# Tokens loaded after the modulation weights, and the first normalisation done by halves of the tokens, in a one-core hybrid attention and expert block

## The chip, the cores and the metric

The kernel runs on one core of a Trainium2 chip. The metric is the device time of the program in microseconds (us), the median of several executions. PE is TensorE, DVE is VectorE, ACT is ScalarE, POOL is GpSimd and SP is SyncE, which only issues DMAs here.

## The reference

The program is one residual block on 1024 tokens of width 1024: a LayerNorm of the input, a modulation by a vector `c`, a mixer (delta-rule linear attention beside sliding-window attention), and a mixture of experts. The change lies in the first lines of it and in the key columns of the first projection:

```python
h = layer_norm(x, ln_in_g, ln_in_b)
ada = jax.nn.silu(c) @ w_ada[l] + b_ada[l]
sh1, sc1, gt1, sh2, sc2, gt2 = jnp.split(ada, 6, axis=-1)
u = h * (1.0 + sc1[:, None, :]) + sh1[:, None, :]
proj = u @ w_in                # k_b: the 128 key columns of the window attention
```

`layer_norm` takes mean and variance over the 1024 channels of each token, so a token's normalised row needs nothing of other tokens.

## The kernel before

The program is a row of stages (`prepare`, `attention`, `project`, `delta_rule`, `merge`, `route`, `experts`). Each stage is a block with one hand-written instruction list for each engine; at its end all engines meet at a barrier. The change touches `prepare` alone.

`prepare` makes `u`, the modulated tokens, transposed (channels on the partitions) and as a sum of two float16 numbers, high and low, in `m.u`. Its work:

- SP issues all loads on one queue: a small table, the vectors, the tokens `x` in four pieces of two token chunks (1 MB each, L270), the first 2048 columns of `w_ada` in five pieces (three of 2 MB, two of 1 MB, L272), the first slice of the dense weights (`load_dense(…, 0)`, L170 with 1 MB and L171 with 16 columns in 64-byte runs), small rows, the rest of the table and the second dense slice. A token chunk is 128 tokens, one a partition.
- DVE takes the moments of the eight token chunks (`bn_stats` L390, two for each chunk, `bn_aggr` L393), ACT the square root (L355), DVE reciprocal and shift (L396, L398), and ACT normalises the eight chunks in place (L359, counted in `z_ok`).
- The modulation: PE multiplies `silu(c)` with the columns 0 to 1023 of `w_ada` as the pieces land (`ada(k)`, L295), DVE sums the columns 1024 to 2047 into `part` (L404, L407). PE turns both into columns (L335, L302), and DVE makes scale and shift `m.mod` (L414 to L421, `ada_ok`).
- The loop of 16 steps, n = 0 to 15. In step n PE transposes four 128x128 blocks into a PSUM bank (`turn(n)`, L311): eight channel groups k by two halves of the tokens, of 512 each. A bank serves four steps, so `turn(n)` waits until step n-4 has been read (`hi_ok`). ACT reads the bank of an even step twice (L371, L373) and makes the high part of an odd step (L377) from what DVE read (L427). DVE then subtracts to get the low part of either (L433, `ut_ok`). PE multiplies the key columns with the result, three matmuls a step (`keys(n)`, L321). PE's order is `turn(n)`, `keys(n-4)`, `turn(n+1)`, `keys(n-3)` and so on. Before, n goes over both halves of one k and then the next k, and turns 0 to 2 stand between `ada(5)` and `ada(6)`.
- ACT and DVE split the first dense slice into high and low (L182, L190); `keys(0)` waits for the low part. DVE does it after step 1.
- At n = 8 PE also makes the rows of the relative bias (L346); DVE copies them after step 9, and SP stores them for `attention`.

`attention` begins behind the barrier with PE's value products (L559), which need all of `u`.

Of the kernel before, what the change touches and what calls it, by code (L numbers as in the profile page):

```python
# [11 lines left out]
ALU = mybir.AluOpType  # L12
ACT = mybir.ActivationFunctionType
# [211 lines left out]
def prepare(nc, m, a):  # L225
# [4 lines left out]
    with ExitStack() as ctx:  # L230
# [33 lines left out]
        @block.sync  # L264
        def _(sp):
            sp.dma_start(m.table[:, 0:2 * P], a["table"][:, 0:2 * P]).then_inc(table_in, 16)
            sp.dma_start(vec_rows[:], a["vectors"]).then_inc(vecs_in, 16)
            sp.dma_start(conv_rows[:], a["conv_rows"]).then_inc(vecs_in, 16)
            for c in range(4):
                sp.dma_start(x[:, 2 * c:2 * c + 2, :], x_view[:, 2 * c:2 * c + 2, :]).then_inc(x_in[c], 16)  # L270
            for n, ks in enumerate(GROUPED):
                sp.dma_start(wada[:, ks[0]:ks[-1] + 1, :], w_view[:, ks[0]:ks[-1] + 1, 0:2 * D]).then_inc(wada_in[n], 16)  # L272
            load_dense(m, a, sp, 0)
            sp.dma_start(m.small[:], a["small"].to_broadcast([P, 72])).then_inc(small_in, 16)
            sp.dma_start(rel[:], a["rel_bias"]).then_inc(rel_in, 16)
            sp.dma_start(m.table[:, 2 * P:], a["table"][:, 2 * P:]).then_inc(rest_in, 16)
            load_dense(m, a, sp, 1)
            sp.wait_ge(bias_rows, 1)
            sp.dma_start(m.bias_dram.rearrange("i h x -> h i x"), rel_rows[:].rearrange("h (o x) -> h o x", o=1).to_broadcast([QH, COPIES, 320])
                         ).then_inc(m.bias_out, 16)  # L280
            sp.wait_ge(small_in, 16)
            sp.wait_ge(m.bias_out, 16)

        @block.tensor
        def _(pe):
            pe.wait_ge(table_in, 16)
            pe.wait_ge(vecs_in, 32)
            pe.transpose(ps[:, 0, 0:VEC_N], vec_rows[:], m.const("ident")[0:VEC_N, 0:VEC_N])
            pe.transpose(ps[:, 0, VEC_N:VEC_N + 96], conv_rows[:], m.const("ident")[0:96, 0:96]).then_inc(vecs_t, 1)
            pe.wait_ge(vecs_ok, 1)  # L290

            def ada(k):
                pe.wait_ge(wada_in[k // 2 if k < 6 else k - 3], 16)
                for n in range(ON_TENSOR):
                    last = pe.matmul(ps[0:1, ROW[n], :], m.silu_c[:, k:k + 1], wada[:, k, n * 512:(n + 1) * 512], start=(k == 0), stop=(k == KC - 1))  # L295
                    if k == KC - 1:
                        last.then_inc(ada_mm, 1)

            def columns(n):
                pe.wait_ge(row_ok[n], 1)  # L300
                for j in range(4 * n, 4 * n + 4):
                    last = pe.transpose(ps[:, 6, j:j + 1], ada_row[0:1, j * P:(j + 1) * P], m.const("ident")[0:1, 0:1])  # L302
                last.then_inc(cols_mm, 1)

            def turn(n):

                k, half = n // 2, n % 2
                if n >= 4:
                    pe.wait_ge(hi_ok, n - 3)
                for c in range(4):  # L310
                    last = pe.transpose(ps[:, 2 + n % 4, c * P:(c + 1) * P], x[:, 4 * half + c, k * P:(k + 1) * P], m.const("ident"))  # L311
                last.then_inc(zt, 1)

            def keys(n):

                k, half = n // 2, n % 2
                if n == 0:
                    pe.wait_ge(m.w_lo, 4)
                pe.wait_ge(ut_ok, n + 1)
                for t, (wp, up) in enumerate(PASSES):  # L320
                    last = pe.matmul(ps[:, half, :], m.w16[:, 0, wp, k, 0:P], m.u[:, up, k, half * 512:half * 512 + 512],  # L321
                                     start=(k == 0 and t == 0), stop=(k == KC - 1 and t == 2))
                if k == KC - 1:
                    last.then_inc(m.k_mm, 1)

            pe.wait_ge(silu_ok, 1)
            for k in range(KC):
                ada(k)
                if k == KC - 3:
                    pe.wait_ge(z_ok, TC)  # L330
                    for n in range(3):
                        turn(n)
            pe.wait_ge(part_ok, 1)
            for j in range(KC):
                last = pe.matmul(ps[:, 6, KC + j:KC + j + 1], part[:, j * P:(j + 1) * P], m.const("ones")[:, 0:1], start=True, stop=True)  # L335
            last.then_inc(cols_mm, 1)
            for n in range(ON_TENSOR):
                columns(n)
            turn(3)
            for n in range(4, 2 * KC):  # L340
                turn(n)
                keys(n - 4)
                if n == 8:
                    pe.wait_ge(rel_in, 16)
                    pe.wait_ge(rest_in, 16)
                    pe.matmul(ps[0:QH, 7, 0:320], rel[:], m.const("one_hot", BUCKETS), start=True, stop=True).then_inc(bias_mm, 1)  # L346
            for n in range(2 * KC - 4, 2 * KC):
                keys(n)

        @block.scalar  # L350
        def _(act):
            act.wait_ge(vecs_ok, 1)
            nc.scalar.activation(sig_c[:], m.vec("c"), ACT.Sigmoid).then_inc(sig_ok, 1)
            act.wait_ge(var_ok, 1)
            nc.scalar.activation(std[:], mv[:, :, 1], ACT.Sqrt, bias=eps[:, 0:1]).then_inc(std_ok, 1)  # L355

            act.wait_ge(shift_ok, 1)
            for c in range(TC):
                nc.scalar.activation(x[:, c, :], x[:, c, :], ACT.Identity, scale=rstd[:, c:c + 1], bias=shift[:, c:c + 1]).then_inc(z_ok, 1)  # L359
            act.wait_ge(ada_mm, 1)  # L360
            nc.scalar.copy(ada_row[:, 0:512], ps[0:1, ROW[0], :]).then_inc(row_ok[0], 1)
            split_dense_high(nc, m, act, 0)

            act.wait_ge(ada_ok, 1)
            for n in range(2 * KC):
                k, half = n // 2, n % 2
                if half == 0:
                    act.wait_ge(zt, n + 1)
                    if n >= 4:
                        act.wait_ge(ut_ok, n - 3)  # L370
                    nc.scalar.activation(u32[:, n % 4, :], ps[:, 2 + n % 4, :], ACT.Identity,  # L371
                                         scale=m.mod[:, 0, k:k + 1], bias=m.mod[:, 1, k:k + 1]).then_inc(u32_even, 1)
                    nc.scalar.activation(m.u[:, 0, k, 0:512], ps[:, 2 + n % 4, :], ACT.Identity,  # L373
                                         scale=m.mod[:, 0, k:k + 1], bias=m.mod[:, 1, k:k + 1]).then_inc(hi_ok, 1)
                else:
                    act.wait_ge(u32_odd, k + 1)
                    nc.scalar.copy(m.u[:, 0, k, 512:T], u32[:, n % 4, :]).then_inc(hi_ok, 1)  # L377

        @block.vector
        def _(dve):  # L380
# [3 lines left out]
            nc.vector.tensor_copy(m.vecs[:], ps[:, 0, 0:VEC_N + 96]).then_inc(vecs_ok, 1)  # L384
            dve.wait_ge(sig_ok, 1)
            nc.vector.tensor_tensor(m.silu_c[:], sig_c[:], m.vec("c"), ALU.mult).then_inc(silu_ok, 1)
            for c in range(TC):
                dve.wait_ge(x_in[c // 2], 16)
                for s in range(2):
                    step(nc.vector.bn_stats(stats[:, c, s, :], x[:, c, s * 512:(s + 1) * 512]))  # L390
            step.settle()
            for c in range(TC):
                last = nc.vector.bn_aggr(mv[:, c, :], stats[:, c, :, :])  # L393
            last.then_inc(var_ok, 1)
            dve.wait_ge(std_ok, 1)
            step(nc.vector.reciprocal(rstd[:], std[:]))  # L396
            step.settle()
            nc.vector.scalar_tensor_tensor(shift[:], mv[:, :, 0], -1.0, rstd[:], ALU.mult, ALU.mult).then_inc(shift_ok, 1)  # L398

            for k in range(KC):  # L400
                dve.wait_ge(wada_in[k // 2 if k < 6 else k - 3], 16)
                piece = wada[:, k, ON_TENSOR * 512:]
# [17 lines left out]
            step.settle()  # L420
            nc.vector.tensor_tensor(m.mod[:, 1, :], m.mod[:, 1, :], ada[:, 0:KC], ALU.add).then_inc(ada_ok, 1)  # L421
            dve.wait_ge(ada_ok, 1)
            for n in range(2 * KC):
                k, half = n // 2, n % 2
                if half == 0:
                    dve.wait_ge(zt, n + 2)
                    nc.vector.tensor_scalar(u32[:, n % 4 + 1, :], ps[:, 3 + n % 4, :], m.mod[:, 0, k:k + 1], m.mod[:, 1, k:k + 1],  # L427
                                            ALU.mult, ALU.add).then_inc(u32_odd, 1)
                    dve.wait_ge(u32_even, k + 1)
                else:  # L430
                    dve.wait_ge(u32_odd, k + 1)
                dve.wait_ge(hi_ok, n + 1)
                nc.vector.tensor_tensor(m.u[:, 1, k, half * 512:half * 512 + 512], u32[:, n % 4, :], m.u[:, 0, k, half * 512:half * 512 + 512],  # L433
                                        ALU.subtract).then_inc(ut_ok, 1)
                if n == 1:
                    split_dense_low(nc, m, dve, 0)
                if n == 9:
                    dve.wait_ge(bias_mm, 1)
                    nc.vector.tensor_copy(rel_rows[:], ps[0:QH, 7, 0:320]).then_inc(bias_rows, 1)
# [2176 lines left out]
```

## Time and profile before

| | us |
|---|---|
| three runs | 2009.5, 2012.44, 2005.38 |
| median | 2009.5 |
| the profiled execution | 2011.88 |
| its span, first to last instruction | 2010.0 |
| PE busy / DVE busy / ACT busy | 1830.9 / 1441.6 / 1066.0 |
| last key product of `prepare` starts its run of 15 | 63.66 |
| first value product of `attention` | 67.70 |

Times of the trace count from the start of the span. `prepare` is the first 67 us of it. A row of the trace's timeline has start, length, engine, line, operation, tiles and count, and in brackets how long the engine was idle before and what ended that.

### The profile page before, as it was taken

What the parts mean: (1) busy time and instruction counts of PE and PEld (TensorE: products, weight loads), DVE (VectorE), ACT (ScalarE), POOL (GpSimd) and SP (SyncE); (2) the same over time, 40 slices, a digit from 0 to 9 for tenths busy, and PEclk for the clock granted to TensorE, in tenths of its full rate; (3) what the DMA queues carried; (4) which work ended last, traced back from release to release, by engine and by line L of the source; (5) the groups of instructions that cost most, each with busy time, mean ns of one, the idle gap of its engine ahead of it and who ended that gap; (6) DMA issues with size and microseconds to landing.
All of it is one profiled execution on the core that took longest, in us unless ns stands there. A gap on an engine that the chain in (4) does not pass through costs nothing. (4 is left out here: it accounts for less than half of the span.)

```text
span 2010.0 us, 35245 instructions
## 1 busy us (share of the span) xinstructions
PE 1830.9 (91%) x14108; PEld 1041.1 (52%) x14108; DVE 1441.6 (72%) x1820; ACT 1066.0 (53%) x1292; POOL 358.7 (18%) x230
## 2 busy tenths in 40 slices
PE   4988869999978999989999999379999999999965
PEld 1655554444448999964444455334444444444432
DVE  5455555777776666627575778779999888888938
ACT  3455552355343334324333411169889888888944
POOL 0000000111101122100000000024444444444410
PEclk9999979999999999999999999589999999999988
DMA  8500007573545313006223221379999999999935
GB/s 318 101 22 22 1 1 282 189 251 126 179 107 128 81 50 93 7 14 189 77 80 94 75 81 73 130 292 409 403 406 410 403 394 401 391 396 384 383 135 207
DMA packets 161716, 391.32 MB, mean 195 GB/s; under 512 B 25371, under 2 KB 102804, under 8 KB 132910
## 3 DMA queue, kind: packets, MB, share of 16 engines
q1 hardware_dynamic: 146574, 357.87, 49.2%
q0 software_dynamic: 15008, 31.56, 4.1%
q8 instruction: 96, 1.57, 0.3%
q14 instruction: 38, 0.31, 0.1%
HBM read 361.68 MB, written 48.68 MB: 204 GB/s over the span
## 5 line engine op out<-in xcount | busy, mean ns | idle before, releaser
L2268 PE MATMUL ps<-w_gate_up_split,gathered_t 128*128 128x512 f16 x1728 | 387.8, 381 | 8.0 <-ACT gathered_t L2342 3.8
L2434 DVE SCALAR_TENSOR_TENSOR w_gate_up_split<-w_staged,w_gate_up_split 128x2048 f16<-128x2048 f32 x144 | 327.5, 2289 | 56.1 <-ACT w_gate_up_split L2333 55.0
L2333 ACT ACTIVATE w_gate_up_split<-w_staged 128x2048 f16<-128x2048 f32 x144 | 274.2, 1908 | 66.5 <-PEq L144 31.4
L2268 PEld LDWEIGHTS ps<-w_gate_up_split,gathered_t 128*128 128x128 f16 x1728 | 167.3, 98 | 209.0 <-ACT gathered_t L2342 10.5
L219 PE MATMUL ps<-u_transposed,w_gates_split 128*128 128x512 f16 x1152 | 253.9, 382 | 5.0 <-PEq L144 3.0
L825 PE MATMUL ps<-u_transposed,w_dense_split 128*128 128x512 f16 x1152 | 250.5, 379 | 1.8 <-DVE w_dense_split L190 1.0
L2295 PE MATMUL ps<-w_down_split,hidden_t 128*128 128x512 f16 x864 | 193.8, 381 | 7.8 <-ACT hidden_t L2379 4.7
L219 PEld LDWEIGHTS ps<-u_transposed,w_gates_split 128*128 128x128 f16 x1152 | 113.1, 98 | 145.5 <-issue 13.0
L825 PEld LDWEIGHTS ps<-u_transposed,w_dense_split 128*128 128x128 f16 x1152 | 111.9, 98 | 142.4 <-issue 7.1
L2434 DVE SCALAR_TENSOR_TENSOR w_down_split<-w_staged,w_down_split 128x2048 f16<-128x2048 f32 x72 | 164.2, 2289 | 21.1 <-ACT w_down_split L2333 20.8
L2333 ACT ACTIVATE w_down_split<-w_staged 128x2048 f16<-128x2048 f32 x72 | 137.1, 1907 | 46.1 <-DMA w_staged<-in_w_down 30.3
L2295 PEld LDWEIGHTS ps<-w_down_split,hidden_t 128*128 128x128 f16 x864 | 82.9, 98 | 104.3 <-ACT hidden_t L2379 6.5
L190 DVE SCALAR_TENSOR_TENSOR w_dense_split<-w_dense_ring,w_dense_split 128x512 f16<-128x512 f32 (+2 forms) x29 | 41.0, 1413 | 109.7 <-ACT w_dense_split L182 109.7
L1348 ACT ACTIVATE level_product<-ps 128x256 f32<-128x256 f32 x80 | 30.7, 384 | 145.8 <-PE ps L1223 143.8
L2224 POOL DMA_INDIRECT slots_scratch<-block_output,slot_row_now x36 | 49.1, 1365 | 327.4 <-ACT block_output L2351 319.0
L1737 ACT ACTIVATE gate_sigmoids<-ps 128x1024 f32<-128x1024 f32 x24 | 24.5, 1023 | 143.0 <-PE ps L219 143.0
L498 PE MATMUL ps<-u_transposed,w_dense_split 128*128 128x512 f16 x384 | 90.0, 380 | 0.0
L952 DVE SCALAR_TENSOR_TENSOR delta_output<-w_gates_split,vector_columns,delta_output 128x1024 f32<-128x1024 f32 x66 | 83.8, 1283 | 7.2 <-ACT delta_output L888 5.6
L1671 PE MATMUL ps<-w_out_split,delta_output 128*128 128x512 f16 x384 | 84.0, 379 | 0.0
L2210 POOL DMA_INDIRECT gathered<-u_scratch,slot_token_now x34 | 76.9, 2263 | 29.0 <-POOL slot_token_now L2207 29.0
L1085 POOL DMA_DIRECT2D qkv_scratch<-delta_output x20 | 11.1, 553 | 392.5 <-ACT delta_output L895 392.5
L2220 POOL COPY slot_row_now<-slot_rows_index 128x1 uint32 (+1 forms) x36 | 76.6, 2128 | 0.1
(364 smaller groups left out, 2934.7 us busy)
## 6 DMA issues: line engine op xcount, KB each, us to landing
w_staged<-in_w_gate SPq DMA_DIRECT2D x72, 1024.0 KB, 12.2
w_staged<-in_w_up SPq DMA_DIRECT2D x72, 1024.0 KB, 11.6
w_staged<-in_w_down SPq DMA_DIRECT2D x72, 1024.0 KB, 12.0
w_dense_ring<-in_w_in SPq DMA_DIRECT2D x17, 1024.0 KB, 7.6
w_ada_ring<-in_w_ada SPq DMA_DIRECT2D x8, 2048.0 KB
w_gates_ring<-in_w_in SPq DMA_DIRECT2D x24, 512.0 KB, 6.4
qkv_scratch<-delta_output POOLq DMA_DIRECT2D x20, 512.0 KB, 4.0
attention_output<-qkv_scratch SPq DMA_DIRECT2D x8, 1024.0 KB, 5.9
```

The lines of the kernel that those rows point to most:

```text
L219: last = pe.matmul(m.ps[:, 2 * j + half, :], m.gate16[n % 2][:, j, wp, k, :], m.u[:, up, k, half * 512:half * 512 + 512], start=(t == 0), ...
L498: last = pe.matmul(ps[:, bank, :], w16[:, i % 2, wp, k, (j % 2) * P:(j % 2 + 1) * P], m.u[:, up, k, half * 512:half * 512 + 512], start=(t ...
L825: last = pe.matmul(ps[:, 2 * b + half, :], w16[:, (FIRST + p) % 2, i, k, b * P:(b + 1) * P], m.u[:, j, k, half * 512:half * 512 + 512], st ...
L952: last = nc.vector.scalar_tensor_tensor(acc[:, b, :], raw[:, b, 1 + t:1 + t + T], conv[:, t, n:n + 1], acc[:, b, :], ALU.mult, ALU.add)
L1671: last = pe.matmul(ps[:, y_bank(c) + half, :], merged(k, op)[:, c * P:(c + 1) * P], m.w_out[:, wp, k, half * 512:half * 512 + 512], start= ...
L2210: pool.indirect_dma_start(xg[:, s].rearrange("p h d -> p (h d)"), None, m.u2_dram.rearrange("t h d -> t (h d)"), bass.IndirectOffsetOnAxis ...
L2220: nc.gpsimd.tensor_copy(row[:, s:s + 1], m.slot_row[:, bass.ds(n, 1)]).then_inc(S("row_ready"), 1)
L2224: pool.indirect_dma_start(m.y_dram, bass.IndirectOffsetOnAxis(ap=row[:, s:s + 1], axis=0), y[:, s, :], None, bounds_check=2 * T - 1, oob_i ...
L2268: last = pe.matmul(ps[:, GU[s] + j, :], xt[:, s, xp, k, :], w16[:, j, wp, k, :], start=(k == 0 and t == 0), stop=(k == KC - 1 and t == 2))
L2295: last = pe.matmul(ps[:, 6 + half, :], ht[:, s, hp, k, :], wd16[:, wp, k, half * 512:half * 512 + 512], start=(k == 0 and t == 0), stop=(k ...
L2333: nc.scalar.activation(split(kind, 0, int(q)), staged(m, kind, int(q)), ACT.Identity, scale=W_SCALE).then_inc(hi_ok[kind + q], 1)
L2434: nc.vector.scalar_tensor_tensor(split(kind, 1, int(q)), staged(m, kind, int(q)), W_SCALE, split(kind, 0, int(q)), ALU.mult, ALU.subtract) ...
```

## The change

The loads are issued in another order: `w_ada`, the first dense slice, then the tokens. PE does all of `ada(k)` without turns between them. Moments, square root, shift and normalising are done for token chunks 0 to 3 and again for chunks 4 to 7. The loop's steps run over k for the first half of the tokens (n = 0 to 7) and then over k for the second half (n = 8 to 15); the moments of the second half stand on DVE before step 2, its square root on ACT before step 4, its shift on DVE and its normalising on ACT before step 6. `turn(0)` waits for four normalised chunks, `turn(8)` for eight. The split of the first dense slice stands before the loop on DVE.

```diff
@@ sync
-            for c in range(4):
-                sp.dma_start(x[:, 2 * c:2 * c + 2, :], x_view[:, 2 * c:2 * c + 2, :]).then_inc(x_in[c], 16)
             for n, ks in enumerate(GROUPED):
                 sp.dma_start(wada[:, ks[0]:ks[-1] + 1, :], w_view[:, ks[0]:ks[-1] + 1, 0:2 * D]).then_inc(wada_in[n], 16)
             load_dense(m, a, sp, 0)
+            for c in range(4):
+                sp.dma_start(x[:, 2 * c:2 * c + 2, :], x_view[:, 2 * c:2 * c + 2, :]).then_inc(x_in[c], 16)
@@ tensor
             def turn(n):
-                k, half = n // 2, n % 2
+                k, half = n % KC, n // KC
+                if k == 0:
+                    pe.wait_ge(z_ok, 4 * (half + 1))
...
             for k in range(KC):
                 ada(k)
-                if k == KC - 3:
-                    pe.wait_ge(z_ok, TC)
-                    for n in range(3):
-                        turn(n)
...
-            turn(3)
+            for n in range(4):
+                turn(n)
@@ scalar
-            act.wait_ge(var_ok, 1)
-            nc.scalar.activation(std[:], mv[:, :, 1], ACT.Sqrt, bias=eps[:, 0:1]).then_inc(std_ok, 1)
...
+            def tokens(half):
+                act.wait_ge(shift_ok, half + 1)
+                for c in range(4 * half, 4 * half + 4):
+                    nc.scalar.activation(x[:, c, :], x[:, c, :], ACT.Identity, scale=rstd[:, c:c + 1], bias=shift[:, c:c + 1]).then_inc(z_ok, 1)
...
             split_dense_high(nc, m, act, 0)
+            roots(0)
+            tokens(0)
             act.wait_ge(ada_ok, 1)
             for n in range(2 * KC):
-                k, half = n // 2, n % 2
-                if half == 0:
+                k, half = n % KC, n // KC
+                if n == 4:
+                    roots(1)
+                if n == 6:
+                    tokens(1)
+                if n % 2 == 0:
@@ vector
+            moments(0)
+            shifts(0)
+            split_dense_low(nc, m, dve, 0)
             for n in range(2 * KC):
-                k, half = n // 2, n % 2
-                if half == 0:
+                k, half = n % KC, n // KC
+                if n == 2:
+                    moments(1)
+                if n == 6:
+                    shifts(1)
+                if n % 2 == 0:
...
-                if n == 1:
-                    split_dense_low(nc, m, dve, 0)
```

SP's queue, from the fourth load on (`attention_output` is the tile that holds the tokens here). Before:

```order
L270 DMA attention_output<-in_x 128x2x1024 x4
L272 DMA w_ada_early<-in_w_ada 128x2x2048 x3
L272 DMA w_ada_early<-in_w_ada 128x2048 x2
L170 DMA w_dense_ring<-in_w_in 128x8x256
L171 DMA w_dense_ring<-in_w_in 128x8x16
L274 DMA small_rows<-in_small 128x72
```

Now:

```order
L270 DMA w_ada_early<-in_w_ada 128x2x2048 x3
L270 DMA w_ada_early<-in_w_ada 128x2048 x2
L170 DMA w_dense_ring<-in_w_in 128x8x256
L171 DMA w_dense_ring<-in_w_in 128x8x16
L273 DMA attention_output<-in_x 128x2x1024 x4
L274 DMA small_rows<-in_small 128x72
```

The four token loads have moved behind seven others.

DVE, around the moments. Before, they stand ahead of the modulation's partial sums:

```order
L386 TENSOR_TENSOR silu_c<-sigmoid_c,vector_columns 128x8
L390 BN_STATS ln_stats<-attention_output 128x6 x16
L393 BN_AGGR ln_mean_var<-ln_stats 128x2 x8
L396 RECIPROCAL ln_rstd<-ln_std 128x8
L398 SCALAR_TENSOR_TENSOR ln_minus_mean_rstd<-ln_mean_var,ln_rstd 128x8
L404 TENSOR_SCALAR ada_early_partial<-w_ada_early,silu_c 128x1024
L407 SCALAR_TENSOR_TENSOR ada_early_partial<-w_ada_early,silu_c,ada_early_partial 128x1024 x7
L412 COPY ada_early_row<-ps 1x512
```

Now, behind the modulation, from the first half's moments into the loop:

```order
L400 BN_STATS ln_stats<-attention_output 128x6 x8
L403 BN_AGGR ln_mean_var<-ln_stats 128x2 x4
L409 RECIPROCAL ln_rstd<-ln_std 128x4
L411 SCALAR_TENSOR_TENSOR ln_minus_mean_rstd<-ln_mean_var,ln_rstd 128x4
L190 SCALAR_TENSOR_TENSOR w_dense_split<-w_dense_ring,w_dense_split 128x2176
L448 TENSOR_SCALAR u_float<-ps,modulation 128x512
L454 TENSOR_TENSOR u_transposed<-u_float,u_transposed 128x512 x2
L400 BN_STATS ln_stats<-attention_output 128x6 x8
L403 BN_AGGR ln_mean_var<-ln_stats 128x2 x4
L448 TENSOR_SCALAR u_float<-ps,modulation 128x512
L454 TENSOR_TENSOR u_transposed<-u_float,u_transposed 128x512 x2
L448 TENSOR_SCALAR u_float<-ps,modulation 128x512
```

L448 and L454 are the loop's operations (L427 and L433 before); eight moments of the second half now stand inside it, after one pair of steps.

ACT, the loop. Before, all eight chunks are normalised ahead of it (L359):

```order
L355 ACTIVATE ln_std<-ln_mean_var,ln_eps 128x8
L359 ACTIVATE attention_output<-attention_output,ln_minus_mean_rstd,ln_rstd 128x1024 x8
L361 COPY ada_early_row<-ps 1x512
L182 ACTIVATE w_dense_split<-w_dense_ring 128x2176
L371 ACTIVATE u_float<-ps,modulation 128x512
L373 ACTIVATE u_transposed<-ps,modulation 128x512
L377 CAST u_transposed<-u_float 128x512
```

Now, from the loop's first step:

```order
L380 ACTIVATE u_float<-ps,modulation 128x512
L382 ACTIVATE u_transposed<-ps,modulation 128x512
L386 CAST u_transposed<-u_float 128x512
L380 ACTIVATE u_float<-ps,modulation 128x512
L382 ACTIVATE u_transposed<-ps,modulation 128x512
L386 CAST u_transposed<-u_float 128x512
L356 ACTIVATE ln_std<-ln_mean_var,ln_eps 128x4
L380 ACTIVATE u_float<-ps,modulation 128x512
L382 ACTIVATE u_transposed<-ps,modulation 128x512
L386 CAST u_transposed<-u_float 128x512
L361 ACTIVATE attention_output<-attention_output,ln_minus_mean_rstd,ln_rstd 128x1024 x4
L380 ACTIVATE u_float<-ps,modulation 128x512
```

Four of the eight normalisings now stand inside the loop, after three pairs of steps.

## Rows read from the trace of the kernel before

**Rows 1.** The page: its first line, and the chain that ended last.

```profile
span 2010.0 us, 35245 instructions
...
PE 14%; DMA 12%; DVE 5%; ACT 2%; issue 1%; SPq 0%; ACTq 0%; POOLq 0%; DVEq 0%
```

**Rows 2.** Timeline of SP: when each load was issued, and for how long.

```profile
2.04 2.14 SPq L270 DMA_DIRECT2D attention_output<-in_x  x4
4.22 7.71 SPq L272 DMA_DIRECT2D w_ada_early<-in_w_ada  x5
...
13.26 18.71 SPq L171 DMA_DIRECT2D w_dense_ring<-in_w_in  x1
32.01 4.05 SPq L274 DMA_DIRECT2D small_rows<-in_small  x1
```

**Rows 3.** Issue to landing of the loads of L270, then L272, then L171.

```profile
DMA to landing us min/median/max: 6.4/9.5/12.6
...
DMA to landing us min/median/max: 16.9/25.4/27.2
...
DMA to landing us min/median/max: 26.0/26.0/26.0
```

**Rows 4.** Timeline of DVE: moments, dense split, and one step of the loop.

```profile
8.46 10.14 DVE L390 BATCH_NORM_STATS2 ln_stats<-attention_output 128x6 f32<-128x512 f32 x16 [1.00 <-DMA attention_output<-in_x]
...
18.64 0.71 DVE L393 BATCH_NORM_AGGREGATE ln_mean_var<-ln_stats 128x2 f32<-128x12 f32 x8
...
45.83 2.42 DVE L190 SCALAR_TENSOR_TENSOR w_dense_split<-w_dense_ring,w_dense_split 128x2176 f16<-128x2176 f32 x1
...
57.35 0.81 DVE L427 TENSOR_SCALAR u_float<-ps,modulation 128x512 f32<-128x512 f32 x1 [0.70 <-PE ps L311]
```

**Rows 5.** Timeline of ACT: the normalising, and the loop's first read.

```profile
20.16 9.16 ACT L359 ACTIVATE attention_output<-attention_output,ln_minus_mean_rstd,ln_rstd 128x1024 f32<-128x1024 f32 x8 [0.47 <-DVE ln_minus_mean_rstd L398]
...
43.07 0.78 ACT L371 ACTIVATE u_float<-ps,modulation 128x512 f32<-128x512 f32 x1 [1.67 <-DVE modulation L421]
```

**Rows 6.** Timeline of PE: modulation products, turns and key products.

```profile
21.23 9.57 PE L295 MATMUL ps<-w_ada_early,silu_c 128*1 128x512 f32 x16 [14.59 <-DMA w_ada_early<-in_w_ada]
...
36.08 3.59 PE L295 MATMUL ps<-w_ada_early,silu_c 128*1 128x512 f32 x8
...
48.31 1.46 PE L321 MATMUL ps<-u_transposed,w_dense_split 128*128 128x512 f16 x3 [2.62 <-DVE w_dense_split L190]
49.56 1.06 PE L311 MATMUL ps<-table,attention_output 128*128 128x128 f32 x4
...
51.69 1.06 PE L311 MATMUL ps<-table,attention_output 128*128 128x128 f32 x4
...
58.88 0.60 PE L311 MATMUL ps<-table,attention_output 128*128 128x128 f32 x4
...
59.97 0.60 PE L311 MATMUL ps<-table,attention_output 128*128 128x128 f32 x4
...
63.66 3.72 PE L321 MATMUL ps<-u_transposed,w_dense_split 128*128 128x512 f16 x15
```

**Rows 7.** Groups of DVE from 43 to 67.5 us: count, busy us, mean ns.

```profile
L433 DVE TENSOR_TENSOR u_transposed<-u_float,u_transposed 128x512 f16<-128x512 f32 x16 | 10.9, 688 | 1.8 <-ACT u_transposed L377 0.8 <-ACT u_transposed L373 0.7
L427 DVE TENSOR_SCALAR u_float<-ps,modulation 128x512 f32<-128x512 f32 x8 | 6.5, 806 | 2.5 <-PE ps L311 2.4
```

**Rows 8.** Windows of PE alone: stretch, length, busy (count), granted clock, DMA.

```profile
43.00:44.00 1.00, 0.00 (x0) 0.72 1.00 319
...
53.00:54.00 1.00, 1.00 (x6) 0.66 0.00 0
```

**Rows 9.** Window of all engines, 22 to 23 us: PE first; clock third last.

```profile
22.00:23.00 1.00, 1.00 (x3) 0.24 (x2) 1.00 (x1) 1.00 (x2) 0.00 (x0) 1.00 0.95 393
```

**Rows 10.** Timeline of ACT: its first instruction behind the barrier.

```profile
67.67 0.60 ACT L587 ACTIVATE k_transposed<-ps 128x512 f32<-128x512 f32 x1 [1.97 <-PEq L230]
```

More of the change, by code:

```diff
@@ L353, in _, with roots @@
             nc.scalar.activation(sig_c[:], m.vec("c"), ACT.Sigmoid).then_inc(sig_ok, 1)
-            act.wait_ge(var_ok, 1)
-            nc.scalar.activation(std[:], mv[:, :, 1], ACT.Sqrt, bias=eps[:, 0:1]).then_inc(std_ok, 1)
-            act.wait_ge(shift_ok, 1)
-            for c in range(TC):
-                nc.scalar.activation(x[:, c, :], x[:, c, :], ACT.Identity, scale=rstd[:, c:c + 1], bias=shift[:, c:c + 1]).then_inc(z_ok, 1)
+            def roots(half):
+                cs = slice(4 * half, 4 * half + 4)
+                act.wait_ge(var_ok, half + 1)
+                nc.scalar.activation(std[:, cs], mv[:, cs, 1], ACT.Sqrt, bias=eps[:, 0:1]).then_inc(std_ok, 1)
+            def tokens(half):
+                act.wait_ge(shift_ok, half + 1)
+                for c in range(4 * half, 4 * half + 4):
+                    nc.scalar.activation(x[:, c, :], x[:, c, :], ACT.Identity, scale=rstd[:, c:c + 1], bias=shift[:, c:c + 1]).then_inc(z_ok, 1)
             act.wait_ge(ada_mm, 1)
@@ L362, in _ @@
             split_dense_high(nc, m, act, 0)
+            roots(0)
+            tokens(0)
             act.wait_ge(ada_ok, 1)
             for n in range(2 * KC):
-                k, half = n // 2, n % 2
-                if half == 0:
+                k, half = n % KC, n // KC
+                cols = slice(half * 512, half * 512 + 512)
+                if n == 4:
[3 more added lines that the diff above has]
+                if n % 2 == 0:
                     act.wait_ge(zt, n + 1)
@@ L372, in _ @@
                                          scale=m.mod[:, 0, k:k + 1], bias=m.mod[:, 1, k:k + 1]).then_inc(u32_even, 1)
-                    nc.scalar.activation(m.u[:, 0, k, 0:512], ps[:, 2 + n % 4, :], ACT.Identity,
+                    nc.scalar.activation(m.u[:, 0, k, cols], ps[:, 2 + n % 4, :], ACT.Identity,
                                          scale=m.mod[:, 0, k:k + 1], bias=m.mod[:, 1, k:k + 1]).then_inc(hi_ok, 1)
                 else:
-                    act.wait_ge(u32_odd, k + 1)
-                    nc.scalar.copy(m.u[:, 0, k, 512:T], u32[:, n % 4, :]).then_inc(hi_ok, 1)
+                    act.wait_ge(u32_odd, n // 2 + 1)
+                    nc.scalar.copy(m.u[:, 0, k, cols], u32[:, n % 4, :]).then_inc(hi_ok, 1)
         @block.vector
@@ L386, in _, with moments, shifts @@
             nc.vector.tensor_tensor(m.silu_c[:], sig_c[:], m.vec("c"), ALU.mult).then_inc(silu_ok, 1)
[L387 to L398, printed above, removed]
+            def moments(half):
+                for c in range(4 * half, 4 * half + 4):
+                    dve.wait_ge(x_in[c // 2], 16)
+                    for s in range(2):
+                        step(nc.vector.bn_stats(stats[:, c, s, :], x[:, c, s * 512:(s + 1) * 512]))
+                step.settle()
+                for c in range(4 * half, 4 * half + 4):
+                    last = nc.vector.bn_aggr(mv[:, c, :], stats[:, c, :, :])
+                last.then_inc(var_ok, 1)
+            def shifts(half):
+                cs = slice(4 * half, 4 * half + 4)
+                dve.wait_ge(std_ok, half + 1)
+                step(nc.vector.reciprocal(rstd[:, cs], std[:, cs]))
+                step.settle()
+                nc.vector.scalar_tensor_tensor(shift[:, cs], mv[:, cs, 0], -1.0, rstd[:, cs], ALU.mult, ALU.mult).then_inc(shift_ok, 1)
+            dve.wait_ge(silu_ok, 1)
             for k in range(KC):
@@ L422, in _ @@
             dve.wait_ge(ada_ok, 1)
+            moments(0)
+            shifts(0)
+            split_dense_low(nc, m, dve, 0)
             for n in range(2 * KC):
-                k, half = n // 2, n % 2
-                if half == 0:
+                k, half = n % KC, n // KC
+                if n == 2:
[3 more added lines that the diff above has]
+                if n % 2 == 0:
                     dve.wait_ge(zt, n + 2)
-                    nc.vector.tensor_scalar(u32[:, n % 4 + 1, :], ps[:, 3 + n % 4, :], m.mod[:, 0, k:k + 1], m.mod[:, 1, k:k + 1],
+                    nc.vector.tensor_scalar(u32[:, n % 4 + 1, :], ps[:, 3 + n % 4, :], m.mod[:, 0, k + 1:k + 2], m.mod[:, 1, k + 1:k + 2],
                                             ALU.mult, ALU.add).then_inc(u32_odd, 1)
-                    dve.wait_ge(u32_even, k + 1)
+                    dve.wait_ge(u32_even, n // 2 + 1)
                 else:
-                    dve.wait_ge(u32_odd, k + 1)
+                    dve.wait_ge(u32_odd, n // 2 + 1)
                 dve.wait_ge(hi_ok, n + 1)
```

## The prediction

> **What bounds the kernel now.** I read the page first. The chain that ended last runs through the experts and names nothing of `prepare` [rows 1], so it can't price this change; but it can't excuse it either. `prepare` ends at a barrier, ACT's first instruction behind it waited for PE's queue [rows 10], and from there PE works on `u`. So what `prepare` ends later or earlier moves everything behind it by as much, and the question is where 63.66 + 3.72 = 67.4 us, the end of the last key product [rows 6], goes.
>
> Next I read the queues of the first 67 us. The four token loads were issued from 2.04 us on; the first landed after 6.4 us, at 8.4, the last (issued at 3.5) after 12.6 us, at 16.1 [rows 2, 3], so 1 MB takes 2.55 us. The 8 MB of `w_ada` fill the time until 36.1, where the last products of L295 start [rows 6], and the first dense slice is complete at 13.26 + 26.0 = 39.3 [rows 2, 3]. The tokens' whole preparation hides in that: moments from 8.46 for 10.14 us, normalising from 20.16 for 9.16 us [rows 4, 5], while the weights still arrive. At 39.3 nothing of the tokens is left but transposing. The modulation is ready at 43.07, 3.4 us after the last L295 ends at 39.7, and the loop starts there [rows 5, 6]. It takes 67.4 - 43.1 = 24.3 us, of which DVE is busy 10.9 + 6.5 + 2.4 us [rows 4, 7]. **The bound of `prepare` is bytes until 39.3, then the loop, a ring in which PE, ACT and DVE all take part.**
>
> **The change, part by part.** *The loads.* The bytes are the same, so the tokens and the weights exchange places: with the tokens last they land at 31.7, 34.2, 36.8 and 39.3, counted back from 39.3 by 2.55. The last piece of `w_ada` lands 4 x 2.55 = 10.2 us earlier, at 25.9. One doubt is SP: it sat 18.7 us in issuing the 64-byte runs of L171 and 4.05 in the load behind it, until 36.06, which is when `w_ada` had landed [rows 2]. The token loads now stand behind L171. By the same picture the first is out at about 26, 3 us before its turn comes, so I take no loss; if the queue does run dry, I bound that by one token load, 0 to 2.5 us.
>
> *The modulation.* It is ready at about 27.8 + 3.4 = 31.2, instead of 43.07. That is the gain that the change reaches for. But at 31.2 no token has landed, so it is worth nothing by itself.
>
> *The first half.* Two token loads have landed at 34.2. Four `bn_stats` at 0.63 (10.14 / 16) follow: 36.8. From the first `bn_aggr` to the first normalising took 18.64 to 20.16 = 1.5 us with eight, so 1.2 with four: 38.0. Four normalisings at 1.145 (9.16 / 8): **42.6** [rows 4, 5]. There the loop can begin. That is only 0.5 us ahead of 43.07. DVE's dense split (2.42 us [rows 4]) now lies beside the normalising, costs nothing, and would show only if the normalising were 2 us shorter; before, PE waited 2.62 us for it [rows 6]. That is a gain inside the loop.
>
> *Inside the loop.* Here the other half of the tokens' work now stands, with nothing to hide it. I walk the chain:
> - Turns 0 and 1. PE has been idle since about 31. The turns start 0.9 apart and run 1.06 at the low clock (1.2 GHz), 0.6 at the high one (2.4 GHz) [rows 6, 8]. I take the low one: 44.7.
> - DVE's first pair of steps, 0.81 + 2 x 0.69 = 2.2 [rows 7]: 46.9.
> - The second half's moments, 8 x 0.63 + 4 x 0.09 = 5.4: 52.3. PE runs out of work at about 50, since `keys(2)` needs step 2 of DVE.
> - Pair 2/3, 2.2, then pair 4/5, 2.4 with a wait for ACT: 56.9. ACT's square root (0.3) fits between.
> - Shift on DVE 0.3: 57.2. Then ACT normalises, 4.6: **61.8**. Neither pair 6/7 on ACT nor `turn(8)` on PE can start before; PE, done with `keys(3)` at 55.7, idles 6 us.
> - PE's list then holds `turn(8)`, `keys(4)`, the bias product, `turn(9)`. A turn and its keys start to start are 2.13 us low (49.56 to 51.69) and 1.09 high (58.88 to 59.97) [rows 6]. At the low clock this list takes 2.13 + 1.3 + 1.2 = 4.7: 66.5, and DVE can read the bank.
> - Before, DVE's reading for steps 8 and 9 began at 57.35 [rows 4] and `prepare` ended 10.0 us later. The same steps remain: 76.5, and 0.6 for one more turn at the low clock: **77.1**.
>
> Sum: 77.1 - 67.4 = **+9.7 us**. Within it: start -0.5, dense split out -2.4, moments, shift and normalising in +10.3, the low clock +2 to +3, and small waits for the rest. The profiled execution was 2011.88, so I expect 2021.6 from such a one; the median of the runs shown is 2.4 lower, 2009.5, so the median becomes 2019.2.
>
> *The clock.* The price of the low clock is the least certain term. The granted clock fell at about 43.7, with PE idle from 42.7, and rose at about 53.7, after turns and keys without a gap from 49 on [rows 8]. Two rows disagree on the start. At 22 us the granted clock reads 1.00 after 14.6 us of idle [rows 9], but the sixteen matmuls from 21.23 take 0.60 each where the eight of 36.08 take 0.45 [rows 6]. I believe the matmuls. By the row of the clock alone, PE would be high after any early wait and the sum would be nearer +7. The Trainium skill, "TensorE: Matmul & The Clock Gate", section "Loop structure matters more than you think", says that a long wait for a DMA between matmuls drops PE to the low clock; by it turn 0 and `turn(8)` both start low, as in my sum. It speaks against this change, which adds both waits. The same page says in "Seeing it yourself" that recorded clock events can be unreliable, and the two rows above show such a case.
>
> **The rivals.**
> 1. *The clock stays high behind the 6 us wait at 56 to 62.* `turn(9)` is then done at 64.5 and the end is 74.5: +7.1, or 2016.6. With turns 0 and 1 high too, +6.2. For it: rows 9. Against: the fall at 43.7 after far less.
> 2. *The clock stays low to the end of the loop.* After 66.5, six turns and some eleven groups of key products at 1.04 extra for a turn and its keys, partly hidden by DVE, add 5 to 9 us: +15 to +19, or 2026.5. For it: with steps in half-filled pairs PE has gaps. Against: before, the clock rose while the same list was running [rows 6, 8].
> 3. *Not slower: the tokens land out of the order of issue.* All loads go over one queue and the same 16 engines. If the small rows and the 64-byte runs let the token loads overtake, so that they land 5 us before my times, the first half starts at 37.6, and each step up to the 61.8 follows by 5: +4.7, or 2014.2. It decides from about 4 us earlier on, when the rest is under 6.0 us. For it: SP's long issue of L171 [rows 2] shows that the queue doesn't take all loads alike. Against: the loads of L270 and L272 landed one behind the other at an even pace [rows 3]. The Trainium skill, "DMA: Bandwidth & Descriptors", section "Queues, rings and completion order", says that completion is not in order of issue for DMAs that use few engines; by it this could happen only beside a load of few engines.
> 4. *The reorder doesn't do what it says: SP holds the token loads back* behind L171, so that the queue runs dry by 2.5 to 5 us. Every step after moves with it: +12.2 to +14.7, or 2023.
>
> **How the numbers follow.** A measurement of this kernel can tell about 0.3% from no change, which is 6.0 us: slower means over 2015.5. Chances: my forecast (+9.7) 0.52, rival 1 0.20, rival 2 0.10, rival 3 0.08, rival 4 0.10. The three runs shown spread by 7 us, so a median can stray by 2 to 3. Forecast, 2 and 4 give slower nearly always, rival 1 in two of three cases, rival 3 hardly. That makes slower 0.77, same 0.21, and 0.02 for faster, since no row lets the loop both start earlier and lose its stalls. The likeliest time is 2019.2. The range runs from rival 1 less 2.6 of spread, 2014.0, to rival 4 with some spread, 2026.0; it leaves out most of rival 2 and part of rival 3.
>
> **What would show it.** Right: `w_ada`'s last landing near 26 and the tokens' last near 39.3; the modulation at about 31; the first turn at 42.6 and not before; between it and the barrier a stretch of DVE `bn_stats` (about 47 to 52) and one of ACT normalising (57 to 62) with PE idle in both; the first L559 at about 77.4 instead of 67.7. Behind that, stages of the same length as before. Wrong: a first turn well before 42; the turn behind ACT's normalising in 0.6 us instead of 1.06; a barrier before 73; or a later stage that takes the delay in.

## The result, and the profile after

| | before | changed |
|---|---|---|
| median of six runs, us | 2012.99 | 2022.42 |
| range of the six | 2005.38 to 2015.13 | 2020.65 to 2025.8 |
| profiled execution / its span | 2011.88 / 2010.0 | 2023.0 / 2021.1 |
| first key copy of ACT behind the barrier | 67.67 | 77.66 |

The ratio is 1.005, with a 95% interval of 1.0037 to 1.0063: the change makes the kernel slower by 9.4 us, where 9.7 were forecast. The runs of before have moved as well: its median of six is 3.5 us above that of the first three, so 2022.42 stands higher than the 2019.2 of the forecast although the difference is right.

SP's timeline of the changed kernel (start, length, engine, line, what is loaded, count):

```profile
2.04 2.59 SPq L270 DMA_DIRECT2D w_ada_early<-in_w_ada  x5
4.67 0.47 SPq L170 DMA_DIRECT2D w_dense_ring<-in_w_in  x1
5.18 14.83 SPq L171 DMA_DIRECT2D w_dense_ring<-in_w_in  x1
20.05 7.95 SPq L273 DMA_DIRECT2D attention_output<-in_x  x4
```

From issue to landing, the token loads of L273:

```profile
DMA to landing us min/median/max: 8.7/11.2/12.3
```

The last token load was issued at 27.3 and landed at 39.6 (27.3 + 12.3). Before, the last byte of the dense slice landed at about that time, 39.3 [rows 2, 3]. The loads have only changed places. DVE's timeline shows what each load released:

```profile
25.67 1.28 DVE L421 SCALAR_TENSOR_TENSOR ada_early_partial<-w_ada_early,silu_c,ada_early_partial 128x1024 f32<-128x1024 f32 x1 [1.03 <-DMA w_ada_early<-in_w_ada]
...
30.82 0.17 DVE L435 TENSOR_TENSOR modulation<-modulation,ada_early 128x8 f32<-128x8 f32 x1
32.05 4.96 DVE L400 BATCH_NORM_STATS2 ln_stats<-attention_output 128x6 f32<-128x512 f32 x8 [1.06 <-DMA attention_output<-in_x]
...
45.69 1.50 DVE L454 TENSOR_TENSOR u_transposed<-u_float,u_transposed 128x512 f16<-128x512 f32 x2
47.11 4.84 DVE L400 BATCH_NORM_STATS2 ln_stats<-attention_output 128x6 f32<-128x512 f32 x8
...
63.08 1.29 DVE L454 TENSOR_TENSOR u_transposed<-u_float,u_transposed 128x512 f16<-128x512 f32 x2 [5.38 <-ACT u_transposed L382]
66.36 0.81 DVE L448 TENSOR_SCALAR u_float<-ps,modulation 128x512 f32<-128x512 f32 x1 [1.99 <-PE ps L313]
```

The modulation is ready at 31.0 (30.82 + 0.17), 12 us earlier than before [rows 5], and nothing can use it yet. The second `bn_stats` row is the second half's moments between two steps of the loop. ACT's timeline has the normalisings, the second one inside the loop too:

```profile
38.24 4.63 ACT L361 ACTIVATE attention_output<-attention_output,ln_minus_mean_rstd,ln_rstd 128x1024 f32<-128x1024 f32 x4 [0.44 <-DVE ln_minus_mean_rstd L411]
44.14 0.78 ACT L380 ACTIVATE u_float<-ps,modulation 128x512 f32<-128x512 f32 x1 [1.26 <-PE ps L313]
...
57.02 4.63 ACT L361 ACTIVATE attention_output<-attention_output,ln_minus_mean_rstd,ln_rstd 128x1024 f32<-128x1024 f32 x4 [1.11 <-DVE ln_minus_mean_rstd L411]
```

PE's timeline answers to [rows 6]:

```profile
42.93 4.53 PE L313 MATMUL ps<-table,attention_output 128*128 128x128 f32 x20 [12.84 <-ACT attention_output L361]
...
53.74 0.82 PE L323 MATMUL ps<-u_transposed,w_dense_split 128*128 128x512 f16 x3 [3.61 <-DVE u_transposed L454]
...
61.70 1.11 PE L313 MATMUL ps<-table,attention_output 128*128 128x128 f32 x4 [6.06 <-ACT attention_output L361]
62.61 1.49 PE L323 MATMUL ps<-u_transposed,w_dense_split 128*128 128x512 f16 x3
...
73.96 3.40 PE L323 MATMUL ps<-u_transposed,w_dense_split 128*128 128x512 f16 x15
77.68 12.28 PE L578 MATMUL ps<-w_dense_split,u_transposed 128*128 128x144 f16 x192 [0.32 <-PEq L230]
```

PE waits three times: 12.84 us for the first half of the tokens, 3.61 for DVE's moments, 6.06 for ACT's second normalising. The first wait is the earlier modulation, unused. It costs little against before, since the loop's first read on ACT is at 44.14 where it was at 43.07 [rows 5]. The other two carry the result. Before, PE waited in the loop for 2.62 us [rows 6] and 1.85 us:

```profile
44.57 1.11 PE L311 MATMUL ps<-table,attention_output 128*128 128x128 f32 x4 [1.85 <-ACT u_transposed L373]
```

The granted clock of the changed kernel, in windows of PE (length, busy, granted clock, DMA share, GB/s; 0.50 is 1.2 GHz, 1.00 is 2.4 GHz, and a value between them is a window in which it changed):

```profile
54.00:56.00 2.00, 1.64 (x10) 1.00 0.00 0
56.00:58.00 2.00, 0.00 (x0) 1.00 0.00 0
58.00:60.00 2.00, 0.00 (x0) 0.65 0.00 0
60.00:62.00 2.00, 0.29 (x2) 0.50 0.00 0
...
66.00:68.00 2.00, 2.00 (x8) 0.50 0.00 0
68.00:70.00 2.00, 2.00 (x12) 0.79 0.03 6
```

It falls at about 58.6, in the last wait, and the turns and keys from 61.70 to about 68.8 run at 1.2 GHz.

The last product of `prepare` ends at 77.36 against 67.38, +9.98 us. Behind the barrier the delay stays: the first load of the expert weights, on SP, starts at

```profile
1283.20 0.81 SPq L2099 DMA_DIRECT2D w_staged<-in_w_gate  x2
```

which is 8.9 us later than before (1274.34).

### The profile page after: what moved, and what is told of

It is laid out like the page before. It is cut to its first block and busy times, and to the rows that moved or that the text cites. A ratio compares the mean times of both kernels' runs of the same rounds, so it can differ in the third digit from the quotient of the medians.

```text
span 2021.1 us, 35250 instructions
## 1 busy us (share of the span) xinstructions
PE 1834.0 (91%) x14108; PEld 1043.6 (52%) x14108; DVE 1441.3 (71%) x1822; ACT 1066.0 (53%) x1293; POOL 356.7 (18%) x230
## 5 line engine op out<-in xcount | busy, mean ns | idle before, releaser
L1104 POOL DMA_DIRECT2D qkv_scratch<-delta_output x20 | 11.1, 553 | 401.4 <-ACT delta_output L914 401.4
L621 ACT ACTIVATE scores_biased<-scores_biased,softmax_rows 128x192 f32<-128x192 f32 x128 | 56.5, 446 | 37.9 <-DVE softmax_rows L671 37.9
```

Source lines behind the costliest of these rows:

```text
L621: nc.scalar.activation(sp_[:, t % 2, h, :], sp_[:, t % 2, h, :], ACT.Exp, bias=neg_max[:, t % 2, h:h + 1], accum_out=sums[:, t % 2, h:h + 1])
```

## The experiments

Places in `prepare` are compared by the start of attention's first value product: 67.70 before, 77.68 in the changed kernel.

### The second half ahead of the loop

```diff
 act:     roots(0)
          tokens(0)
+         roots(1)
+         tokens(1)
          for n in range(2 * KC):
-             if n == 4: roots(1)
-             if n == 6: tokens(1)
 dve:     split_dense_low(nc, m, dve, 0)
+         moments(1)
+         shifts(1)
          for n in range(2 * KC):
-             if n == 2: moments(1)
-             if n == 6: shifts(1)
```

> The changed kernel, loads still with the tokens last, but the second half's moments, root, shift and normalising stand ahead of the loop on DVE and ACT. Theory A (what costs is the second half's work standing inside the loop, DVE 5.4 us and ACT 4.6 us in a chain that PE waits for): moments of the second half from 40.5 to 46, normalised at 50.7, the loop's first read near 51, then pairs of steps every 2.2 to 2.5 us; first value product of attention at 68 to 70 against 77.7, so +0.5 to +2.5 us against the kernel before, within 0.3%. Theory B (what costs is that the tokens land last, 23 us later than before): the time stays with the changed kernel, first value product at 76 to 78, +8 to +10 us. Theory C (the low clock behind the 6 us wait is the larger part): the wait is gone, so it can't be told from A by the sum, but A wants the second half's 10 us to vanish from the loop, C only 3 us: 74 to 75.

Measured: 1.0024 of before (1.0014 to 1.0033), median 2018.32. PE's timeline of this run:

```profile
42.58 3.68 PE L313 MATMUL ps<-table,attention_output 128*128 128x128 f32 x16 [12.75 <-ACT attention_output L361]
52.20 1.11 PE L313 MATMUL ps<-table,attention_output 128*128 128x128 f32 x4 [5.95 <-ACT u_transposed L380]
...
70.94 12.28 PE L574 MATMUL ps<-w_dense_split,u_transposed 128*128 128x144 f16 x192 [0.32 <-PEq L230]
```

Same loads, same work, 6.7 us less. Theory B, that late tokens cost all of it whatever the lists do, falls. So does C as the main part: a wait of 5.95 us is still there, ahead of 52.20, with the low clock behind it (the turn took 1.11 us), and the 6.7 us are back all the same. I had written that this wait would be gone, and had left the low clock out of A's number, which came out 0.9 us too low. What is left of the loss against the kernel before is 3.2 us.

### Only the moments ahead

```diff
 dve:     split_dense_low(nc, m, dve, 0)
+         moments(1)
+         shifts(1)
          for n in range(2 * KC):
-             if n == 2: moments(1)
-             if n == 6: shifts(1)
 act:     roots(0)
          tokens(0)
+         roots(1)
          for n in range(2 * KC):
-             if n == 4: roots(1)
```

> The changed kernel with the second half's moments, root and shift ahead of the loop, the normalising of the second half still on ACT before step 6. Theory A: the moments no longer stop DVE inside the loop (5.4 us), but PE still waits for the normalising; first value product at 69.3 if PE's clock stays high behind that wait of about 4 us, at 73 if it drops; so -4.5 to -8.4 us against the changed kernel. Theory B: no more than 1 us less than the changed kernel, since the tokens land as late.

Measured: 1.0021 (1.0011 to 1.0031), first value product at 71.26. That is 6.4 us less than the changed kernel, between A's two ends. PE's wait for the normalising has shrunk from 6.06 us:

```profile
57.04 0.66 PE L313 MATMUL ps<-table,attention_output 128*128 128x128 f32 x4 [2.79 <-ACT attention_output L361]
...
58.99 1.12 PE L313 MATMUL ps<-table,attention_output 128*128 128x128 f32 x4
```

The turn behind the wait is at the high clock (0.66), the next one at the low (1.12), so the clock fell just after. Of the pair, the moments are the dear part: with them and the square root out of the loop, the normalising costs 0.3 us more inside it than ahead of it (71.26 against 70.94), and the two ratios, 1.0021 and 1.0024, can't be told apart.

### Filler in the 6 us wait

```diff
                 turn(n)
                 keys(n - 4)
+                if n == 7:
+                    for _ in range(24):
+                        pe.matmul(ps[:, 6, :], m.w16[:, 0, 0, 0, 0:P], m.u[:, 0, 0, 0:512], start=True, stop=True)
```

> The changed kernel with 24 float16 matmuls into an unused bank put on PE behind the key products of step 3, where it waits 6 us for the second half (they add no work that anybody reads). They take about 5.2 us. Theory C and my sum: the clock stays high at 61.7, turn(8) to turn(9) take 2.4 us less and the next turns 0.5: first value product at 74.3, -3.4 us. If the clock is no part of it: 77.7, no change.

Measured: 1.0039 (1.0024 to 1.0054), first value product at 75.33, -2.35 us against the -3.4 expected. PE's timeline:

```profile
56.56 6.07 PE L344 MATMUL ps<-u_transposed,w_dense_split 128*128 128x512 f16 x24
62.46 0.60 PE L313 MATMUL ps<-table,attention_output 128*128 128x128 f32 x4
...
75.33 12.28 PE L581 MATMUL ps<-w_dense_split,u_transposed 128*128 128x144 f16 x192 [0.32 <-PEq L230]
```

The turn takes 0.60 instead of 1.11, so the clock is a real term. The filler itself took 0.7 us of the gain back: it ran for 6.07 us, not 5.2, since in this execution the clock was low from 54.6 to 58.0, and `turn(8)`, which could have gone at 61.8, started at 62.46.

### The changed lists with the tokens loaded first

```diff
+            for c in range(4):
+                sp.dma_start(x[:, 2 * c:2 * c + 2, :], ...).then_inc(x_in[c], 16)
             for n, ks in enumerate(GROUPED):
                 sp.dma_start(wada[...], w_view[...]).then_inc(wada_in[n], 16)
             load_dense(m, a, sp, 0)
-            for c in range(4):
-                sp.dma_start(x[:, 2 * c:2 * c + 2, :], ...).then_inc(x_in[c], 16)
```

> The changed kernel's instruction lists with the loads in the order of before (tokens, w_ada, dense slice). Theory A, with the moments behind the modulation on DVE and nothing else changed: modulation at about 41.5, moments to 47, first half normalised at 52.4, loop from there with the second half's work in it as in the changed kernel: first value product at 86.7, +9 us against the changed kernel and +19 against the kernel before. Theory B (the late tokens are the cost): it returns to the kernel before, 67 to 70.

Measured: 1.0102 (1.0087 to 1.0117), median 2034.2, first value product at 87.24 where A said 86.7. DVE's timeline shows why:

```profile
41.31 4.84 DVE L400 BATCH_NORM_STATS2 ln_stats<-attention_output 128x6 f32<-128x512 f32 x8
```

PE's timeline has the end of it:

```profile
87.24 12.28 PE L578 MATMUL ps<-w_dense_split,u_transposed 128*128 128x144 f16 x192 [0.32 <-PEq L230]
```

The tokens have been there since 16, but on DVE's list the moments stand behind the modulation, which now ends at 41. Under the changed lists the changed order of loads is worth 9.6 us. The fourth combination, the changed loads under the lists of before, was not run.

### Only the loop's order

```diff
-                k, half = n // 2, n % 2
+                k, half = n % KC, n // KC
```

with the same on PE, ACT and DVE, and nothing else of the change.

> The kernel before with the loop's steps in the changed order alone (all channel groups of the first half, then of the second); loads, norms, split as before. Theory A: the order of the steps in itself costs nothing, as every step has the same work: first value product at 67.7 +- 0.5, same time. If the order costs by itself (the rival that explains the changed kernel by it), up to +10 us.

Measured: 1.0001 (0.9987 to 1.0014):

```profile
66.94 12.28 PE L560 MATMUL ps<-w_dense_split,u_transposed 128*128 128x144 f16 x192 [0.32 <-PEq L230]
```

That is 0.8 us earlier than before, in a profile whose landings are 0.2 us earlier too. The order of the steps costs nothing.

### The split back in the loop

```diff
-            split_dense_low(nc, m, dve, 0)
             for n in range(2 * KC):
...
+                if n == 1:
+                    split_dense_low(nc, m, dve, 0)
```

> The changed kernel with the dense split put back to where it was before, behind step 1 of the loop. My sum counts moving it ahead as a gain of 2.4 us: first value product at 80.0, +2.3 us against the changed kernel. If the split was hidden anyway, 77.7.

Measured: 1.0061 (1.004 to 1.0082) with a median of 2027.17, first value product at 79.48, +1.8 us. PE waits for it again:

```profile
49.34 1.00 PE L323 MATMUL ps<-u_transposed,w_dense_split 128*128 128x512 f16 x3 [2.44 <-DVE w_dense_split L190]
```

So the moved split is a real gain of the change, 1.8 us in place of the 2.4 in my sum.

### Tokens last, arranged as well as I could

```diff
 dve:
-            split_dense_low(nc, m, dve, 0)
             moments(1)
             shifts(1)
+            split_dense_low(nc, m, dve, 0)
 pe:
+            pe.wait_ge(m.w_hi, 4)
             for n in range(4, 2 * KC):
+                if n == 4:
+                    for _ in range(12):
+                        pe.matmul(ps[:, 7, :], m.w16[:, 0, 0, 0, 0:P], m.w16[:, 0, 0, 0:2, 0:2 * P], start=True, stop=True)
                 turn(n)
```

The base is the first experiment.

> The run with the second half ahead of the loop (first value product at 70.94), with the dense split behind the second half's moments instead of before them, and 12 filler matmuls on PE behind turn(3). Split: the second normalising starts 2.4 us earlier. Filler: steps 4 and 5 at the high clock, -1.5 to -2. Together first value product at 67.0 to 68.0, level with the kernel before: tokens last costs nothing then, but gains nothing either. If the late tokens had a price that lists can't hide, it stays at 70 or above.

Measured: 1.0004 (0.9989 to 1.0019), median 2013.58. ACT's timeline has the second normalising right behind the first:

```profile
38.45 4.63 ACT L365 ACTIVATE attention_output<-attention_output,ln_minus_mean_rstd,ln_rstd 128x1024 f32<-128x1024 f32 x4 [0.44 <-DVE ln_minus_mean_rstd L413]
44.40 4.63 ACT L365 ACTIVATE attention_output<-attention_output,ln_minus_mean_rstd,ln_rstd 128x1024 f32<-128x1024 f32 x4 [0.44 <-DVE ln_minus_mean_rstd L413]
```

PE's timeline has the end of it:

```profile
68.52 12.28 PE L578 MATMUL ps<-w_dense_split,u_transposed 128*128 128x144 f16 x192 [0.33 <-PEq L230]
```

Of the 10.0 us, 9.2 are back without touching the order of the loads, and the end is 0.5 us later than the latest that I expected. How much of the last 2.4 us is the split's place and how much is the filler was not separated. Being level with the kernel before is also not a fair comparison, because this run has two helps that the kernel before lacks, the split ahead of the loop and the filler. The next run gives both to the kernel before.

### The kernel before, with the split ahead and filler

```diff
 dve:        dve.wait_ge(ada_ok, 1)
+            split_dense_low(nc, m, dve, 0)
             for n in range(2 * KC):
...
-                if n == 1:
-                    split_dense_low(nc, m, dve, 0)
 pe:         for n in range(4, 2 * KC):
+                if n == 4:
+                    (wait for w_hi, 8 filler matmuls into bank 7)
                 turn(n)
+                if n == 4:
+                    (10 filler matmuls into bank 7)
                 keys(n - 4)
```

> The kernel before (its loads and its norms), with DVE's split of the first dense slice ahead of the loop and 8 + 10 filler matmuls on PE between turn(3), turn(4) and keys(0), into a bank that nobody reads. It tries for more than either kernel has: the loop without the low clock and with a shorter wait of keys(0). If the clock stays high from 42.7 on: first value product of attention at 64.2 against 67.70, -3.5 us, -0.17%. [...]

Measured: 0.9977 (0.9963 to 0.999), median 2009.86 against 2012.03 of before on the same chip. PE's timeline:

```profile
42.66 3.44 PE L344 MATMUL ps<-w_dense_split 128*128 128x512 f16 x8
45.93 0.60 PE L311 MATMUL ps<-table,attention_output 128*128 128x128 f32 x4
...
65.29 12.28 PE L565 MATMUL ps<-w_dense_split,u_transposed 128*128 128x144 f16 x192 [0.32 <-PEq L230]
```

This beats both kernels, by 2.4 us against the kernel before in the trace and 2.2 in the medians. Two windows of PE show the granted clock:

```profile
42.00:44.00 2.00, 2.00 (x10) 0.59 0.99 332
44.00:46.00 2.00, 2.00 (x7) 0.55 0.01 3
```

So the low clock is not gone. It fell at about 42.4, with PE busy, and rose at about 45.8, where in the kernel before it rose at 53.7. The first eight fillers ran mostly at the low clock (3.44 us, 0.43 each), and `turn(4)` started 1.4 us later than before (45.93 against 44.57). That this is the missing 1.1 us of the 3.5 is likely but not shown. The two edits of this run were not separated.

With the same two helps, tokens first (65.29, median 2009.86) stands 3.2 us ahead of tokens last (68.52, median 2013.58) in the traces, and 3.7 us in the medians, as it stood 3.2 us ahead in the first experiment. The filler is not placed alike in the two. But the traces show where late tokens still tell: with tokens last the second half is normalised at 49.03 (44.40 + 4.63), and only then does ACT begin the loop. I found no arrangement in which tokens last wins.

## Why the prediction was right

| step | forecast | measured |
|---|---|---|
| last piece of `w_ada` | 25.9 | 25.67 |
| modulation ready | 31.2 | 31.0 |
| first half normalised | 42.6 | 42.87 |
| DVE done with pair 0/1 | 46.9 | 47.2 |
| second half's moments done | 52.3 | 52.4 |
| second half normalised | 61.8 | 61.65 |
| DVE reads the bank of step 9 | 66.5 | 66.36 |
| end of the last key product | 77.1 | 77.36 |

The walk fits at every step, so the mechanism came out and not only the total. Some terms in the list under the sum were off; they follow below.

**The loads.** They went as the sum had it. The issue of the first token load took until 25.7 (20.05 + 5.69), behind L171, and from there to 38 the DMA engines were busy in every window of 2 us. The four loads landed at 32.0, 34.5, 37.0 and 39.6, each 0.2 to 0.3 us behind its forecast and in the order of issue. Rival 4 had its cause there, but no price. Rival 3, landing out of order, did not happen.

**The loop.** Every step of the walk is within 0.4 us. What carries it is that the second half's work stood in a chain through DVE, ACT and PE. The first experiment took only that out of the chain and got back 6.7 us with the tokens still last; the seventh, with the split moved and the filler added, got back 9.2. From DVE's reading for step 9 to the end took 11.0 us (66.36 to 77.36) where the walk had 10.6, since the clock rose only at about 68.8.

**The terms.** The start was not a gain of 0.5 us, as the list of terms under the sum has it. The kernel before had turned its first four steps when the modulation came; in the changed kernel turns 0 and 1 stand behind the normalised half, so ACT's first read came 1.1 us later (44.14 for 43.07) and DVE's 1.9 us later (44.93 for 43.07). The walk had those turns (44.7), and the list hid them in its small waits. The dense split was mis-sized, 1.8 us for 2.4. Moments, shift and normalising took 5.3 + 0.4 + 4.6 = 10.3 us, as forecast. The clock behind the late wait, which rival 1 prices at 2.6 us, came out at 2.35 us with the filler's own 0.7 us against it, so about 3.0, an estimate from the third experiment.

**The clock.** Rival 1, the clock staying high, is refuted in this kernel by the turn of 1.11 us at 61.70, and rival 2, the clock staying low, by its rise at about 68.8. The fall in the kernel before was read as 43.7; the window of 0.72 puts it at about 43.4, with PE idle for only 0.7 us, which makes the case against rival 1 stronger. Two rows disagreed about a start after idle, and I took the low clock, as the matmuls had it. Behind 12.84 us of idle the turns did run at the low clock, and here the granted clock says so as well (0.50 from 32 to 48). The Trainium skill, "TensorE: Matmul & The Clock Gate", section "Loop structure matters more than you think", says that a long wait for a DMA between matmuls brings the low clock. Here the waits were for ACT, and the traces agree at 42.93 and 61.70; behind the 3.61 us at 53.74 the clock stayed high.

**The place behind the barrier.** I said that the delay goes through unchanged. It was 9.98 us at the barrier, 8.9 at the start of the expert weights and 11.1 at the end of the span. The 9.98 us are the change. The differences behind it are of the size by which those stages vary without it: from the first value product to the start of the expert weights they took 1206.6 us before, 1205.5 here and between 1203.1 and 1208.7 in the profiles of the experiments. From there to the end they took 735.7 us before, 737.9 here, and between 735.5 and 739.1 in the experiments, with 739.1 in the kernel before with filler. The code of those stages is the same in all ten. Why they vary was not looked into. So the 9.4 us between the medians, which is so close to the 9.7, owes something to luck; the 9.98 us at the barrier is the firmer confirmation.

## What to carry to other kernels

A load order and the instruction lists of the engines have to be moved together: a value that comes earlier is worth nothing while what it is combined with is still on its way. Before moving work out of a stretch in which engines wait for bytes, ask where it will stand instead; here 10 us of moments and normalising left a stretch of free time and went into the chain of a loop. And if it has to stand there, try the half that is not needed yet ahead of the loop: here that gave 6.7 us, because DVE's stop for the moments and ACT's for the normalising each left PE idle in the ring. When the rearranged kernel comes out level with the old one, give the old one the same helps before calling them equal; here it was then 3.2 us ahead.

## What the runs showed of the hardware that was not expected

- The granted clock in the trace may not be right near the start of the program. In windows of PE in the changed kernel, both stretches read 1.00, with the DMA engines equally busy, but half as many of the same matmuls fit in the first:

```profile
12.00:14.00 2.00, 2.00 (x3) 1.00 1.03 434
14.00:16.00 2.00, 2.00 (x6) 1.00 1.00 422
```

  The Trainium skill, "TensorE: Matmul & The Clock Gate", section "Seeing it yourself", warns that recorded clock events can be unreliable, and this looks like a case of it. That the clock was really low there is argued from the matmuls; no run tested another cause.

- The same wait does not always lower the clock. With PE idle from about 50.1 to 53.7 in the changed kernel the clock stayed high until 58.6, about 3 us into the next wait. In the run with filler, the same list up to there, PE was idle for 3.95 us and the clock fell at about 54.6, after PE had started again at 53.86, with keys of step 3 at 1.49 us:

```profile
54.00:56.00 2.00, 2.00 (x9) 0.65 0.00 0
56.00:58.00 2.00, 2.00 (x6) 0.50 0.00 0
58.00:60.00 2.00, 2.00 (x11) 1.00 0.00 0
```

  In the kernel before it fell at about 43.4, 0.7 us into a wait. So the length of the wait by itself did not tell, in these traces, whether and when the clock fell.

- A small load can hold its issuing engine for long. L171 moves 64 KB in 64-byte runs and held SP for 14.83 us here and 18.71 before [rows 2], behind other queued loads; the five loads of 8 MB ahead of it took 2.59 us to issue. The short runs are not the only suspect, since the loads behind it were held as well (the first token load for 5.69 us, L274 before for 4.05), and the runs and the full queue were not separated. In this kernel it had no price, since SP's next loads were still in time.
